# Sample attention over a gathered list of the kept keys, and layer-1 modulation in three column groups

## What is computed

```python
def adaln(c, w, b):
    return jnp.split(jax.nn.silu(c) @ w + b, 6, axis=-1)      # 9 rows x 1024 by 1024 x 6144

def dsa_sample(q, k_new, v_new, qi, ki_new, wi, cache_k_l, cache_v_l, cache_ki_l, page_table):
    ...
    topk = min(TOPK_MAX, L // 4)                                # 256 of 2049 keys
    ki_past = cache_ki_l[page_table].reshape(DB, past, IDX_DIM)
    ki_all = jnp.concatenate([ki_past, ki_new.astype(ki_past.dtype)], axis=1)
    sc = indexer_scores(qi, wi, ki_all, q_pos, jnp.arange(L))
    _, idx = lax.top_k(sc, topk)
    ...
    k_sel = jnp.where(is_new, gather_rows(k_new, nidx), cache_k_l[phys, off])
    v_sel = jnp.where(is_new, gather_rows(v_new, nidx), cache_v_l[phys, off])
    return sparse_attend(q, k_sel, v_sel, valid)                # soft maximum over the 256 keys, times v
```

## Time and profile before

| | us |
|---|---|
| median of 3 runs | 6386.84 |
| lowest and highest run | 6369.41 to 6388.28 |
| profiled execution | 6381.06 |
| its span, first to last instruction | 6379.3 |
| mean granted clock of TensorE | 0.854 of full |

### The profile page before, as it was taken

One profiled execution on the slowest core, in us unless ns is written; L12 is line 12 of the kernel. 1 busy time (PEld: TensorE's weight loads), 2 busy tenths in 40 slices (PEclk: granted clock), 3 DMA queues, 4 the chain that ended last, 5 costly groups with the idle time before them and its releaser, 6 DMA issues. The chain is left out here.

```text
span 6379.3 us, 58455 instructions
## 1 busy us (share of the span) xinstructions
PE 4882.5 (77%) x16452; PEld 2506.2 (39%) x16453; DVE 2275.0 (36%) x5015; ACT 1870.2 (29%) x3244; POOL 699.7 (11%) x900
## 2 busy tenths in 40 slices
PE   7999356777889998887675599936888886569980
PEld 2444122223333333333234444415565564534440
DVE  1111464445445546643122310134444442331105
ACT  0111134455666552221121122212222231212222
POOL 0111210000000000111221000120000000200013
PEclk9999577788999999998885699967898896579995
DMA  6111100000000000005342677771100100437865
GB/s 241 57 50 41 49 19 12 12 12 12 5 12 12 12 12 12 17 14 196 110 137 97 260 280 283 256 285 50 40 20 20 39 13 12 157 124 256 303 236 201
DMA packets 177186, 634.11 MB, mean 99 GB/s; under 512 B 28920, under 2 KB 47737, under 8 KB 157930
## 3 DMA queue, kind: packets, MB, share of 16 engines
q1 hardware_dynamic: 116764, 425.22, 19.0%
q0 software_dynamic: 39072, 131.90, 5.9%
q10 hardware_dynamic: 21184, 75.03, 2.9%
HBM read 497.41 MB, written 134.72 MB: 99 GB/s over the span
## 5 line engine op out<-in xcount | busy, mean ns | idle before, releaser
L2142 PE MATMUL experts_ps_gu<-w_sb,experts_xT 128*128 x1504 | 679.3, 606 | 43.9 <-DMA w_sb<-moe_w_in 39.4
L997 PE MATMUL attend_po<-attend_PT,V 128*128 128x512 f32 x1088 | 572.1, 652 | 8.9 <-ACT attend_total L742 8.9
L2659 PE MATMUL recurrent_psAB<-recurrent_hT,rec_w_in_sb 128*128 128x256 f32 (+1 forms) x2304 | 537.4, 393 | 10.6 <-ACT recurrent_hT L2454 10.6
L769 ACT ACTIVATE attend_passed<-attend_score,attend_cand 128x1024 bf16<-128x1024 f32 (+8 forms) x279 | 439.4, 1575 | 357.1 <-DVE attend_cand L869 333.3
L469 PE MATMUL project_pj<-project_w,project_hT 128*128 128x512 f32 (+2 forms) x1360 | 507.4, 531 | 6.6 <-ACT project_proj L385 5.5
L2659 PEld LDWEIGHTS recurrent_psAB<-recurrent_hT,rec_w_in_sb 128*128 128x128 f32 x2304 | 465.2, 216 | 76.7 <-issue 11.7
L1007 PE MATMUL attend_aux<-attend_hide,attend_identb 128*128 128x512 bf16 (+3 forms) x640 | 246.8, 389 | 291.0 <-DVE attend_mx L812 241.1
L812 DVE TENSOR_REDUCE attend_mx<-attend_aux 128x1 f32<-128x512 f32 (+3 forms) x640 | 365.2, 606 | 278.1 <-PE attend_aux L1008 270.7
L2142 PEld LDWEIGHTS experts_ps_gu<-w_sb,experts_xT 128*128 128x128 f32 x1504 | 285.4, 195 | 372.7 <-issue 372.7
L732 ACT ACTIVATE attend_PT<-attend_big 128x512 f32<-128x512 f32 x544 | 292.2, 588 | 366.0 <-PE attend_big L986 365.3
L2132 PE MATMUL experts_ps_y<-w_sb,experts_midT 128*128 x752 | 342.9, 599 | 11.4 <-issue 11.4
(11 more groups left out here) (425 smaller groups left out, 6132.3 us busy)
## 6 DMA issues: line engine op xcount, KB each, us to landing
w_sb<-moe_w_in SPq DMA_DIRECT2D x64, 2048.0 KB, 11.4
w_sb<-moe_w_in SPq DMA_DIRECT2D x64, 1024.0 KB, 8.8
yb_scratch<-experts_y ACTq DMA_DIRECT2D x94, 512.0 KB, 8.6
index_slab<-ada_w_in SPq DMA_DIRECT2D x12, 2048.0 KB, 12.1
sample_V<-cache_v_in POOLq DMA_DIRECT2D x128, 128.0 KB, 2.4
sample_K<-cache_k_in SPq DMA_DIRECT2D x128, 128.0 KB
route_x<-xa_scratch SPq DMA_DIRECT2D x32, 512.0 KB, 4.6
hs_scratch<-route_h ACTq DMA_DIRECT2D x32, 512.0 KB, 4.8
```

What stands on the lines that cost most here:

```text
L769: act.activation(passed[:, 0:L[m]], score[:, m % 2, 0:L[m]], ACT.Sign, bias=threshold, accum_out=balance[:, :]).then_inc(balanced, 1)
L997: pe.matmul(po[:, n % 2, :], V1[:, b, n, :], PT[:, g % 4, :], start=(b == 0), stop=(b == S[i] // NKV - 1)).then_inc(pv_done, 1)
L2142: last = pe.matmul(ps_gu[:, u, :], xT[:, u, k, :], w1[:, bass.ds(slot, 1), k, :].rearrange("p a n -> p (a n)"), start=(k == 0), stop=(k == ...
L2659: last = pe.matmul(psAB[:, c % 2, part, 0:W], w_in[:, k, part * D + c * P:part * D + (c + 1) * P], hT[:, k, 0:W], start=(k == 0), stop=(k ...
```

## The change

**A list instead of a mask.** In the index phase `same`'s block constant becomes a tile that is kept for both phases (`pick_blk`), with two new ones, `pick_idx` (for each sequence 256 row numbers of the cache, in 2 columns of 128 partitions) and `pick_hide`. After the threshold VectorE makes `taken` (1 for a kept key), TensorE and a scan number the kept keys of each sequence (`rank`), and the ranks are turned so that column c holds the ranks of the keys at offset c of all 128 pages. Then for each of the 128 offsets VectorE writes `marks`, 128x256 in bf16 (1 where the place equals the rank), and TensorE multiplies it by 16 columns of `values` (for each sequence the offset and the page number), adding up 128 products in one PSUM tile; two transposes and one VectorE step make row numbers of it. `hide_s` and its transfers are gone.

**Attention over the list.** GpSimd gathers the 256 kept rows of K and of V of all 8 sequences, 32 gathers of 128 rows. A sequence has 2 blocks of 128 keys and the new key as column 256 of the scores; the queries of all sequences are laid out on a skew (`qm`, 128 columns of which 16 are not zero), so that all 8 sequences' scores are added in one tile of 128x257, with one maximum, one exponent and one sum. The values' product adds 16 blocks and the new keys' in one tile. The output stays on the chip (`o_s` is gone).

**Modulation.** The eight weight slices of a column block are spread over three groups of 32 columns of TensorE, with `cond` (32 columns, 9 of them used) in place of `condT`; ScalarE copies the three partial results, and one more matmul (`same_row`) adds them. A step of the generator is now a bias matmul, a set of three, three or two, or the addition: 59 steps. One step follows each count, and one every fourth mark.

```diff
@@ sample index, GpSimd, VectorE
+                pool.iota(offset_i[:, :], pattern=[[0, NS * NPAGE]], base=0, channel_multiplier=1).then_inc(consts, 1)
+                pool.iota(places_i[:, :], pattern=[[1, TOPK]], base=0, channel_multiplier=0).then_inc(consts, 1)
+                pool.memset(values[:, :], 0.0).then_inc(consts, 1)
...
-                dve.wait_ge(consts, 8)
+                dve.wait_ge(consts, 11)
...
+                    if g == 0:
+                        dve.tensor_copy(places[:, :], places_i[:, :])
+                    elif g == 1:
+                        dve.tensor_copy(value_at[:, :, :, 0], offset_i[:, :].rearrange("p (b j) -> p b j", j=NPAGE))
+                    elif g == 2:
+                        dve.tensor_copy(value_at[:, :, :, 1], all_pages[:, :, :])
...
-                dve.tensor_scalar(out, out, -BIG, None, ALU.mult).then_inc(hidden, 1)
+                dve.tensor_scalar(taken[:, :], out, -1.0, 1.0, ALU.mult, ALU.add)
+                dve.drain()
+                dve.tensor_reduce(count[:, :], taken[:, 0:PAGE], AX.X, ALU.add).then_inc(counted_, 1)
+                dve.wait_ge(totalled, 34)
...
+                dve.tensor_tensor_scan(rank[:, :], taken[:, 0:PAGE], taken[:, 0:PAGE], ties[:, 0:1], ALU.add, ALU.bypass)
+                dve.drain()
+                dve.tensor_tensor(rank[:, :], rank[:, :], taken[:, 0:PAGE], ALU.mult).then_inc(ranked, 1)
+                dve.wait_ge(rank_turned, 1)
+                dve.tensor_scalar(rankT[:, :], ps_dot[:, 0, 0:P], -1.0, None, ALU.add)
+                dve.drain()
+                for c in range(P):
+                    if c >= 8:
+                        dve.wait_ge(packed, c - 7)
+                    dve.tensor_scalar(marks[:, c % 8, :], places[:, :], rankT[:, c:c + 1], None, ALU.is_equal).then_inc(marked, 1)
@@ sample index, TensorE
                         for k in range(KC):
-                            last = pe.matmul(ps_mod[0:R, n % 2, :], condT[:, k, :], slab[:, n % SLABS, k, :], start=False, stop=(k == KC - 1))
+                            group = slice(k % 3 * 32, k % 3 * 32 + 32)
+                            last = pe.matmul(ps_mod[group, n % 2, :], cond[:, k, :], slab[:, n % SLABS, k, :],
+                                             start=(0 < k < 3), stop=(k >= KC - 3), tile_position=(0, k % 3 * 32))
...
+                            if k % 3 == 2 or k == KC - 1:
+                                yield
+                        if n:
+                            add_parts(n - 1)
                             yield
+                    add_parts(NMOD - 1)
...
-                    for _ in range(2):
+                    for _ in range(1):
                         next(part, None)
...
+                for c in range(P):
+                    pe.wait_ge(marked, c + 1)
+                    pe.matmul(ps_dot[0:2 * NS, 1, 0:TOPK], values[:, c * 2 * NS:(c + 1) * 2 * NS], marks[:, c % 8, :],
+                              start=(c == 0), stop=(c == P - 1)).then_inc(packed, 1)
+                    if c % 4 == 3:
+                        next(part, None)
@@ sample attention, GpSimd
-                with pool.Fori(0, NS // 2) as j:
...
-                        load_pages(pool, table, T["cache_v"], b, V[:, u], v_in[u])
+                for dst, src, sem_of in ((K, "cache_k", lambda b: k_in[b // 2]), (V, "cache_v", lambda b: v_in)):
+                    rows = T[src].rearrange("a t c -> (a t) c")
+                    for b in range(NS):
+                        for half in range(HALVES):
+                            pool.indirect_dma_start(out=dst[:, b, half, :], out_offset=None, in_=rows,
+                                                    in_offset=bass.IndirectOffsetOnAxis(ap=idx[:, b, half:half + 1], axis=0)).then_inc(sem_of(b), 16)
+                pool.memset(head_in[:, :, :], 1.0).then_inc(head_done, 1)
@@ sample attention, VectorE
+                dve.wait_ge(head_done, 3)
+                dve.tensor_reduce(head_of[:, :], head_in[:, :, :].rearrange("p b n -> p n b"), AX.X, ALU.add)
+                dve.wait_ge(s_dotted, 1)
+                dve.drain()
+                dve.tensor_tensor(s[:, :], ps_s[:, 0:W], hide[:, :], ALU.add)
+                dve.drain()
+                dve.tensor_reduce(negmax[:, :], s[:, :], AX.X, ALU.max, negate=True).then_inc(maxed, 1)
@@ sample attention, TensorE
+                turn_keys(0)
+                for b in range(NS):
+                    if b + 1 < NS:
+                        turn_keys(b + 1)
+                    dots(b)
+                pe.wait_ge(exped, 1)
...
+                pe.wait_ge(pT_ready, 3)
+                pe.wait_ge(v_in, 16 * NS * HALVES)
+                for b in range(NS):
+                    for half in range(HALVES):
+                        pe.matmul(ps_o[:, 0:KV], PT[:, half, b * P:(b + 1) * P], V[:, b, half, :], start=(b == 0 and half == 0), stop=False)
+                pe.matmul(ps_o[:, 0:KV], own_pT[:, :], v_own[:, :], start=False, stop=True).then_inc(pv_done, 1)
```

371 lines of the change are left out of this document (184 added, 187 removed).

## The result

The changed kernel takes 6147.16 us in the median of four runs (6146.96 to 6150.72), the kernel before 6385.18 (6369.41 to 6388.28, four runs too). The medians are 238 us apart; the ratio of the two on record is 0.9633, with a 95% interval of 0.9617 to 0.965. I had forecast 6144 and a range of 6115 to 6195. The profiled execution took 6147.33 us (span 6145.7, mean granted clock 0.853), 233.6 us less of span than the one before.

The account below looks back on a forecast made before the run. Phases closed by all-engine barriers count one for one in the end time; index phase -7 and sample attention -234 make -241 us, from the profiled 6381.06 to 6140, forecast as 6144 since the median lies higher; range 6115 to 6195.

Parts of the forecast that it names:

- Preparation: Index phase before the search: VectorE waits for more GpSimd steps (memset, iotas) and makes three more copies, +3.0 us.
- Search: Index phase, first to last count: VectorE bounds rounds of 1.45 us, three cold ones at 2.5; 48.1 us, -21.3.
- To the marks: Index phase, from the last count to the mark pass: reduction, matmuls, scan, product, transpose and subtraction, 8 us in all.
- Mark pass: Index phase, 128 marks with 28 modulation steps: TensorE 41 us plus 5 for a cold start, VectorE's 37 beside it; 46 us.
- Closing: End of the index phase: copy, two transposes, copy, list and barrier, 3.5 us.
- Sample attention: Phase after the index phase: gathers, scores, values' product, projection and store take 79 us against 312.9, -234.
- rival of slow gathers: Sample attention: 32 gathers of random 1 KB rows at 1.97 instead of 1.25 us, 23 us more, 6167; chance 0.07.
- head mask: Sample attention: VectorE's head mask reduction waits for GpSimd behind all 32 gathers, so the soft maximum starts at 41, not 30.
- drain at the switches: Search and mark pass: each switch between whole-array and column-group matmuls exposes a 0.17 us tail, 14 us more, 6158; chance 0.12.
- lack of concurrency: Search and mark pass: column groups run one behind the other, 43 us more, 6187; chance 0.1.
- gathers in series: Sample attention: each gather is issued after the landing of the other, 323 us for 32, kernel 6424; chance 0.02.
- bad pass: VectorE and TensorE don't overlap over the marks, or clock stays 1.2 GHz in search or pass; 30 to 40 us more, 6179; chance 0.12.

Follow-up runs that it names:

- combined kernel: Changed kernel with four column groups instead of three, a shorter preparation, and V's gathers held for the eighth turned block of K: 6143.26 us, ratio 0.9629.

## Why the prediction was right, and where it was not

**Preparation**: forecast +3.0 us, measured 46.37 - 42.15 = +4.2. The memset and the iotas cost what I said; the load of all pages, which I had left out, does not cost nothing. It lands 0.7 us behind the memset, and both VectorE and TensorE wait for it. The combined kernel takes 3.6 back.

**Search**: forecast 48.1 us, measured 47.7. The bound was right: VectorE's answer sets a warm round. Two sizes were wrong, and that they cancel is luck: the answer takes 1.31 us from count to count where I had 1.41 and took 1.45, and the clock fell back to 1.2 GHz twice after the start, so that eight rounds are 2.03 to 2.37 us long where I had three at 2.5. 23 rounds of 1.31 and these eight make the 47.7. The Trainium skill ("TensorE: Matmul & The Clock Gate", section "Part 3: Packing small matmuls — row/col tiling") gives a speedup of 2.38 for three column tiles, which made, as an estimate, 1.11 us for a step. The trace shows less, at most 1.01 in the search and 0.86 in the mark pass, and decides.

**To the marks**: forecast 8, measured 7.6. **Mark pass**: forecast 46, measured 42.4. TensorE's 41 was the right term; the 5 us for a cold start were too many, and VectorE's 37 is 25. **Closing**: forecast 3.5, measured 4.1.

**Sample attention**: forecast 79, measured 86.8. Gathers 1.25 us apart (rows 8 held for 128 rows of 1 KB, which takes the rival of slow gathers away), K issued by 20.6, V by 40.6, head mask at 41.4: as forecast. The step that did not hold is "TensorE turns and multiplies each K pair as it lands, and is done with the scores at about 30". It holds on one chip (28.1); on the three others, and in the changed kernel's own profile, TensorE's signals came late, the scores were done at 53, and the product with the values starts at 55.9 instead of 44: +11.9. What follows came out shorter: the product 7.2 and not 9.5, with a granted clock of 1.00 behind 7.1 us of work in the 9.3 us ahead of it, and the projection 13.9 and not 15.4, at 1.00 too (0.90 before). Of the 11.9 that leaves about 8. On the chip without late signals attention took 75.7, below my 79; but that kernel has the head mask first, so V, landed at 42.7, decides in it. The changed kernel itself did not run there. With its mask at 41.4, and the 2.65 us from the score sum to the product, it would start the product at about 44, as forecast (an estimate).

**Rivals**: drain at the switches is refuted (four marks and a step take 1.30 us in the mark pass with column groups as without, where I had put 0.34 us on top), as is a lack of concurrency, and gathers in series. (The last one's time was added wrong: a phase of 362 us instead of 79 makes 6427, not 6424.) Of the bad pass only the clock came, and in the search. The terms together: index phase 2.7 us too long, attention 7.8 too short, the unchanged phases 2.2 that I had not; and 4 us that I had added for the median. These errors partly cancel: that the total came within 3 us, better than its parts, is luck.

## What to carry to other kernels

Small matmuls with few output rows can be put side by side in column groups at nearly no price in TensorE's time (0.86 us for a step of three groups, as for one matmul). But look at the granted clock of the stretch before and after: it was 0.84 with three groups and 0.64 with four, and the second took the gain back. To find what bounds a loop, vary the work of one side: a round that stays 1.31 us whatever TensorE's step is set by VectorE. A chain that hands over from TensorE to another engine and back should not stand beside a burst of indirect DMAs issued by GpSimd, unless it is short or was seen on more than one chip. When a phase waits for the later of two things, price both: the head mask looked like the wait, and where the signals were late the scores were it.

## What the hardware showed that I had not expected

- TensorE's signals (semaphore increments at the end of a matmul) came up to 24 us late (block 4 of the changed kernel: turned by 3090.94, copied from 3115.43) while GpSimd issued gathers, on three of four chips and in the changed kernel's profile; the last late ones came 2.85 to 2.9 us behind 16 gathers and 5.1 to 5.4 behind 32, whatever the bytes. Other engines' signals were prompt beside them: a score matmul starts 0.05 us behind ScalarE's late copy and 0.06 us behind VectorE's, and VectorE's reduction of the head mask 0.03 us behind GpSimd's last step on it, while the signal of block 4 was still out. On the fourth chip none was late, in three kernels.
- Four column groups of f32, 128 by 32 with 512 columns moving, have records as long as three (1.06 us at the full clock, 1.93 at the low one), and the two records of a single one at the full clock last 1.04 together.
- A VectorE comparison of 256 bf16 elements has a record of 0.28 us and a pitch of 0.197 us.
